# State-space rows, segments and decay products begin in their own group's last two slots; the modulation's multiply-adds one slot sooner in differential heads

## What is computed

```python
# differential attention, one of 8 heads
q = rope(rms_norm(q.reshape(B, S, H, 2, d), q_gain), positions)
k = rope(rms_norm(k.reshape(B, S, H, 2, d), k_gain), positions)
pr = jax.nn.softmax(sc, axis=-1)
w = pr[:, :, 0] - lam * pr[:, :, 1]
o = rms_norm(einsum(w, v), sub_gain) * (1.0 - lam_init)
y = o * jax.nn.silu(gate)
# modulation of the second block
mod = jax.nn.silu(c) @ w + b
# state-space layer, one of 8 groups of heads
acum = jnp.cumsum(ac, axis=1)
decay = jnp.exp(where(causal, acum[:, :, None] - acum[:, None, :], -inf))
y_diag = einsum("blsgk,bsgkp->blgkp", cb[..., None] * decay, xc)
y = (y + xs * D_skip) * jax.nn.silu(z)
yg = yg * rsqrt(mean(square(yg)) + eps)
return y @ out_w
```

## Time and profile before

| | us |
|---|---|
| median of three runs | 3638.04 |
| lowest, highest | 3634.32, 3638.28 |
| the profiled execution, whole | 3631.8 |
| its span in the trace | 3630.0 |
| TensorE busy in it | 3492.7 (96%) |
| VectorE busy | 2836.3 (78%) |
| ScalarE busy | 1948.7 (54%) |
| GpSimd busy | 579.3 (16%) |

### The profile page before, as it was taken

How to read it: one execution, slowest core, us unless ns; L and a number is a source line. 1 busy time by engine, 2 the same in 40 slices (tenths; PEclk the granted TensorE clock), 3 DMA queues, 4 the chain that set the end, 5 groups by cost and what they waited for, 6 DMA issues and landing times.

```text
span 3630.0 us, 68468 instructions
## 1 busy us (share of the span) xinstructions
PE 3492.7 (96%) x27986; PEld 3410.1 (94%) x27986; DVE 2836.3 (78%) x4649; ACT 1948.7 (54%) x3084; POOL 579.3 (16%) x546
## 2 busy tenths in 40 slices
PE   7999999999999999999999999999999998999997
PEld 7999999999899989999999999999999997999997
DVE  7787887677787887877877787898989866666665
ACT  6555546566547685565555456554545546434344
POOL 2111112111113011221111112231313300000000
PEclk9999999999999999999999999999999998999998
DMA  6555556434465444656555464445454443555552
GB/s 244 211 196 216 198 222 225 172 151 175 167 274 189 175 157 182 254 180 228 198 219 202 188 251 175 152 156 216 152 209 161 154 151 123 203 204 192 208 193 93
DMA packets 104904, 691.17 MB, mean 190 GB/s; under 512 B 12688, under 2 KB 21008, under 8 KB 22672
## 3 DMA queue, kind: packets, MB, share of 16 engines
q1 hardware_dynamic: 104128, 685.14, 50.9%
q0 software_dynamic: 464, 1.64, 0.1%
HBM read 676.25 MB, written 2.10 MB: 187 GB/s over the span
## 4 chain that ended last, share of the span: by engine, by line
PE 48%; DVE 15%; ACT 5%; issue 3%; POOL 1%; DMA 1%; SPq 0%; DVEq 0%; POOLq 0%; ACTq 0%
PE g L434 14%; PE g L436 14%; PE g L435 14%; DVE w_lo L1457 4%; ACT w_hi L944 2%; DMA scratch<-scratch 1%; POOL scratch L2271 1%; PE turn_bank L473 1%; DVE scratch L1987 1%; DVE con L1987 1%; DVE sq L1951 0%; DVE scratch L1958 0%; DVE sq L1950 0%; PE norm_bank L447 0%; DVE rstd L1950 0%
## 5 line engine op out<-in xcount | busy, mean ns | idle before, releaser
L1457 DVE TENSOR_TENSOR w_lo<-w_raw,w_hi 128x1024 fp32r<-128x1024 f32 x1088 | 1342.9, 1236 | 445.7 <-ACT w_hi L944 433.5
L944 ACT ACTIVATE w_hi<-w_raw 128x1024 fp32r<-128x1024 f32 x1088 | 1134.0, 1054 | 978.1 <-PE g L436 855.2
L434 PE MATMUL g<-p_hi,w_hi 128*128 128x256 f32 x4624 | 1333.0, 288 | 35.0 <-DVE w_lo L1457 23.1
L435 PE MATMUL g<-p_lo,w_hi 128*128 128x256 f32 x4624 | 1310.9, 283 | 0.0
L436 PE MATMUL g<-p_hi,w_lo 128*128 128x256 f32 x4624 | 1310.8, 283 | 0.0
L434 PE MATMUL g<-q_hi,w_hi 128*128 128x256 f32 x3472 | 1004.5, 289 | 18.4 <-DVE scratch L2164 10.5
L436 PE MATMUL g<-q_hi,w_lo 128*128 128x256 f32 x3472 | 986.3, 284 | 0.0
L435 PE MATMUL g<-q_lo,w_hi 128*128 128x256 f32 x3472 | 986.3, 284 | 0.0
L434 PEld LDWEIGHTS g<-p_hi,w_hi 128*128 128x128 f32 x4624 | 889.4, 192 | 49.5 <-DVE w_lo L1457 33.2
L435 PEld LDWEIGHTS g<-p_lo,w_hi 128*128 128x128 f32 x4624 | 889.7, 192 | 1.4
L436 PEld LDWEIGHTS g<-p_hi,w_lo 128*128 128x128 f32 x4624 | 889.2, 192 | 0.0
(11 more groups left out here) (421 smaller groups left out, 3833.1 us busy)
## 6 DMA issues: line engine op xcount, KB each, us to landing
w_raw<-in_slots SPq DMA_DIRECT2D x640, 1024.0 KB, 4.9
scratch<-scratch SPq DMA_DIRECT2D x128, 64.0 KB, 4.9
h<-in_x SPq DMA_DIRECT2D x4, 512.0 KB, 6.3
out_h<-h SPq DMA_DIRECT2D x4, 512.0 KB, 2.6
sq<-in_p POOLq DMA_DIRECT2D x4, 256.0 KB, 3.0
con<-in_consts SPq DMA_DIRECT2D x1, 832.0 KB, 10.9
scratch<-in_distance POOLq DMA_DIRECT2D x1, 576.0 KB, 5.6
vec<-in_vecs SPq DMA_DIRECT2D x1, 383.0 KB, 3.8
```

Source lines behind the costliest of these rows:

```text
L434: pe.matmul(g, wh, hi[:, k], start=n == 0, stop=False)
L435: pe.matmul(g, wh, lo[:, k], start=False, stop=False)
L944: act.activation(w_hi[k % SPLIT][:, cols], raw[MAIN_AT[k] % RAW][:, cols], ACT.Copy).then_inc(hi_ready, 1)
L1457: dve.tensor_tensor(w_lo[k % SPLIT][:, cols], raw[MAIN_AT[k] % RAW][:, cols], w_hi[k % SPLIT][:, cols], SUB).then_inc(lo_ready, 1)
```

## The change

In a differential head the modulation's halves move from the ends of bodies 2, 3, 6, 7 to the ends of bodies 1, 2, 5, 6; `mod_columns` moves from body 1, behind the turn, to body 0, and VectorE takes the columns in body 1 instead of 2. The modulation's blocks of these layers are loaded one place sooner.

In the state-space layer a group's rows, segments, decays and weights of `m = 0, 1` move into its own slots 8 and 9, and those of `m = 2, 3` from the next group's slots 2, 3 to its slots 0, 1. `s_out`, `s_y_out`, the squares and their sums move from steps 2 to 5 to steps 0 to 3, the norm from step 6 to 5, the scaling of y from 7 to 6, its low part from ahead of slot 8 to ahead of slot 7. The wait for the gate's last product at the group's end is taken apart: `s_y_out` waits for the one that it needs. After group 7 the steps beside the projection count from 0.

```diff
-    heads = lambda at: [at + 8 * n + m for n in range(A_HEADS) for m in (2, 6)]
+    heads = lambda at: [at + 8 * n + m for n in range(A_HEADS) for m in (1, 5)]
...
-                if j == 1 and prev:
+                if j == 0 and prev:
                     mod_columns([acc[:]])
...
         def s_previous(g, step, turned):
 
-            if 2 <= step <= 5:
-                s_out(step - 2, turned)
             if step < 4:
-                s_rows(g, step)
-            if step == 6:
+                s_out(step, turned)
+            if step < 2:
+                s_rows(g, step + 2)
+            if step == 5:
                 s_norm()
...
-            if g == S_GROUPS - 1:
-                s_previous(g, 0, None)
+                if n > 7:
+                    s_rows(g, n - 8)
...
         def s_previous(g, step):
+            if step < 2:
+                s_decay(step + 2)
             if step < 4:
-                s_decay(step)
-            if 2 <= step <= 5:
-                s_square(step - 2)
+                s_square(step)
+            if step == 5:
+                factor(rsn[:, 2], "eps_5")
             if step == 6:
-                factor(rsn[:, 2], "eps_5")
-            if step == 7:
                 s_y_hi(g)
...
-                g = take(columns=j == 2 and prev)
+                g = take(columns=j == 1 and prev)
...
-                if j in (2, 3, 6, 7):
-                    ada_half([acc[:]], (j - 2) % 4)
+                if j in (1, 2, 5, 6):
+                    ada_half([acc[:]], (j - 1) % 4)
...
-        def s_y_out(m):
+        def s_y_out(g, m):
 
             dve.wait_ge(yd_done, c.next("yd"))
+            dve.wait_ge(gluon, 10 * g + 7 + m)
...
         def s_previous(g, step):
-            if 2 <= step <= 5:
-                s_y_out(step - 2)
             if step < 4:
-                s_segments(g, step)
-            if step == 7:
+                s_y_out(g, step)
+            if step < 2:
+                s_segments(g, step + 2)
+            if step == 6:
                 s_scale_y(g)
...
-                if g and n == 8:
+                if g and n == 7:
                     s_y_lo(g - 1)
...
+                if n > 7:
+                    s_segments(g, n - 8)
                 if 4 <= n <= 7:
                     s_inputs(g, n - 4)
...
-            if g == S_GROUPS - 1:
-                s_previous(g, 0)
-            dve.wait_ge(gluon, c.at("gluon"))
...
         def s_previous(step):
+            if step < 2:
+                s_weights(step + 2)
             if step < 4:
-                s_weights(step)
-            if 2 <= step <= 5:
-                s_add_square(step - 2)
+                s_add_square(step)
...
+                if n > 7:
+                    s_weights(n - 8)
```

More of the change, by code:

```diff
@@ L799, in s_project @@
                 if tail:
-                    s_previous(S_GROUPS - 1, s + 1, turned)
+                    s_previous(S_GROUPS - 1, s, turned)
                 if s == 4 and i < 2:
@@ L1299, in s_group @@
                     s_previous(g - 1, n)
+                if n > 7:
+                    s_decay(n - 8)
             s_sigmoid(9)
-            if g == S_GROUPS - 1:
-                s_previous(g, 0)
         def s_project(tail=False):
@@ L1307, in s_project @@
                 if tail:
-                    s_previous(S_GROUPS - 1, s + 1)
+                    s_previous(S_GROUPS - 1, s)
         def norm_project(w):
@@ L2399, in s_group @@
                     s_previous(n)
+                if n == 8:
+                    c.next("cb")
+                if n > 7:
+                    s_weights(n - 8)
             s_silu(9)
-            c.next("cb")
         def layer_s():
@@ L2406, in layer_s @@
                 s_group(g)
-            for step in range(6):
+            for step in range(4):
                 s_previous(step)
```

## The result

| | before | after |
|---|---|---|
| median, us | 3638.04 | 3649.28 |
| lowest, highest, us (7 runs each) | 3634.32, 3640.78 | 3647.68, 3654.90 |
| span of the profiled execution, us | 3630.0 | 3645.9 |

The ratio is 1.0033, with a 95% interval of 1.0022 to 1.0044: the change makes the kernel some 12 us slower (11.2 by the medians), which is clear of noise. The time lies in the range given (3627 to 3653), but the forecast was no measurable change, 3641, and the range of the forecast itself ended at 3648. It came out as in the third rival, which had 3649.

A forecast was written before the change was run, and what follows sets the result against it. TensorE, busy 96% of the span, was taken as the bound, so only its waits count. Heads +11.3 and state-space -8.0 gave +3.3 us: 3641 against a median of 3638.04, no measurable change; range with rivals 3627 to 3653.

The forecast's parts named there:

- the third rival: Whole kernel slower: body 5's added half goes through whole, y's scaling eats the state-space gain; 3649 us, chance 0.22.
- The mechanism in the heads: Differential heads: the half entering body 5 delays VectorE's chain to the joined softmax and last scores; heads in all +11.3 us.
- the half taken from body 7: Differential heads, body 7: this modulation half was free, as VectorE idles 1.00 us for `w_hi` afterwards; removing it gains nothing.
- The delay of 0.93 us a head: TensorE's turn waiting for the joined softmax: body 5's added half costs 13.0 us over 14 heads.
- The order of SyncE's queue: Modulation loads in the heads, issued one place sooner: counted as nothing; a late transfer would show as a `w_hi` wait.
- The clock: Differential heads: longer turn waits cause one more fall of TensorE's granted clock, +1.0 us, bounds 0 and 8.
- The gain of the sum over the partitions: Differential heads: `mod_columns` moves ahead of the turn, hiding 0.37 us 14 times in its wait, -5.2 us.
- The state-space gain: Seven state-space groups: shorter VectorE chain, less later start and rows, gains net 1.1 us a group, 8 us in all.
- The start lag: State-space group's slot 0: VectorE's copy starts later behind TensorE, from 0.41 us to about 1.8.
- The chain from there: VectorE in a state-space group, slot 0's copy to slot 6's last scaled inputs: 50.6 us becomes 46.6.
- the segments, the two weight products and the scaling: State-space VectorE chain: segments leaving save 2.62 us, GpSimd weight products leaving save 2.66, scaling of y entering adds 2.15.
- The -0.9: State-space VectorE chain: fewer `w_lo` meetings with GpSimd's sum of squares, and other small ones, -0.9 us, between 0 and -1.6.

The follow-up runs named there:

- the heads alone: Only the differential heads changed, state-space layer as before, against the kernel before: 3647.72 against 3635.31 us, ratio 1.0034.

## Why the prediction was right or wrong

**The mechanism in the heads was right.** The half of the modulation put into body 5 goes through VectorE's chain to the turn and the scores; the last scores wait 10.0 us, as was said, and the turn 20.7 for some 22. Alone the heads cost 12.4 us for a forecast of 11.3. That the half taken from body 7 gained nothing by itself fits the waits, but no run moves it alone.

The delay of 0.93 us a head was 0.85 by the waits at the turn ((20.7 + 5.2 - 14.0) / 14). It also differs from head to head as was said. In the head with 2.43 us of idle time before line 1655 nearly none of it is left (VectorE's timeline after):

```profile
341.91 1.22 DVE L1457 TENSOR_TENSOR w_lo<-w_raw,w_hi 128x1024 fp32r<-128x1024 f32 x1
343.19 0.47 DVE L1655 TENSOR_TENSOR scratch<-scratch,sin_a 128x256 f32<-128x256 f32 x1
```

and the turn behind it waits 1.84 before and 1.44 after (TensorE's timeline, before, then after):

```profile
355.36 0.52 PE L473 MATMUL turn_bank<-con,scratch 128*128 128x128 f32 x3 [1.84 <-DVE scratch L1598]
```

```profile
359.57 0.52 PE L473 MATMUL turn_bank<-con,scratch 128*128 128x128 f32 x3 [1.44 <-DVE scratch L1598]
```

The 0.40 less is the sum over the partitions gone from behind the turn: this head got off, and so did the two others with about 2 us of idle time. After the change nearly every head waits the same 1.44.

**Three terms in the heads were off, and they nearly cancel.** The order of SyncE's queue was counted at nothing, with the words that a late transfer would show as a wait for `w_hi`. It showed as a wait for line 1657 instead: 4.0 us of new waits, and with the heads alone 4.6, none of which is left when the swaps stand ahead of the loads. The clock was given +1.0 for one more fall in the heads; there was none. And the half was rather overrated. Over all heads 14.8 us of idle time in bodies 6 became 0.4, so of 16 x 2.08 = 33.3 up to 18.9 could be left as delay; the heads alone say 12.4 + 5.2 = 17.6 with the queue in it, for 15.5 in the sum, and of these some 7 go when the swaps stand ahead of the loads. The two aren't parted further, for the half also covers part of the swaps' time. The gain of the sum over the partitions (-5.2) holds with the halves of the change (0.44 a head where it was taken as 0.37), and would have been nothing without them.

**The state-space gain was the step that failed**: -8.0, measured +3. In group 5 TensorE goes from slot 0's end to the turn that waits for slot 6's scaled inputs in 49.55 us (48.4 in the sum; before 51.0). The prediction calls this the turn of slot 6; it stands behind slot 7's matmuls, as the matmuls of line 784 right behind it tell, and waits for VectorE to have read the one before it. The stretch and its numbers are the same. The two ends after the change are in PE's timeline:

```profile
2772.18 0.66 PE L748 MATMUL out_bank<-scratch 128*64 128x256 f32 x4
...
2821.73 0.44 PE L473 MATMUL turn_bank<-con,vec 128*128 128x128 f32 x2 [1.97 <-DVE scratch L1976]
```

The start lag was right, 1.8 (2772.18 to the copy at 2773.97). The chain from there was 47.8, not 46.6: of the terms, the segments, the two weight products and the scaling came as said. The -0.9 came too, but not where it was looked for: `w_lo` takes 17.3 us in this stretch before and after, so its meetings with GpSimd did not go, and the 0.9 is smaller idle times and products of VectorE. What the sum lacked were new meetings with GpSimd, whose squares and gate products run beside other operations now: the second step of the convolution took 0.84 instead of 0.49 in two slots, and the first scaling of the inputs 0.83 instead of 0.35 in one slot more. That is 1.2 us. Rows of DVE and POOL in slot 4:

```profile
2805.34 0.83 DVE L1971 TENSOR_SCALAR scratch<-rstd,vec 128x256 f32<-128x256 f32 x1
```

```profile
2804.24 1.77 POOL L2366 TENSOR_TENSOR vec<-vec,sin_b 128x256 f32<-128x256 f32 x1 [2.56 <-ACT sin_b L992]
```

The Trainium skill's SBUF — State Buffer, section Who interferes with whom, lists `tensor_scalar` among the operations that can take the port pair shared with GpSimd, so that the one that comes second is held up. The trace agrees in kind: the operation takes 0.48 us longer beside the gate product, which had 0.67 left. The page's rule had been used in the prediction's sum for the meetings that go, and not for those that come.

The rest was on TensorE: the rows of slots 8 and 9 cost 1.6 us (1.5 in the sum), so that a group gained nothing (69.28 before, 69.48 after from turn to turn). The prediction's own terms say the same: 51.0 - 1.8 - 1.5 leaves no gain from a chain of 47.7 on (it had put this point at 48.0). And two of the waits of 1.98 were followed by a fall of TensorE's clock, which the sum had looked for in the heads and not here:

```profile
2380.00:2385.00 5.00, 4.91 (x27) 4.86 (x28) 4.96 (x9) 2.88 (x5) 1.54 (x1) 0.66 0.20 75
```

It makes the group from 2380 to 2451 1.5 us longer than its neighbours (71.00 for 69.48), and the other fall does the same. From the first group's turn to the last one's it is 2.4 us more than before, and 3.0 of it are these two falls. So of the 8 us forecast nearly all is missing without them, and the falls make the rest of the loss.

**The rival.** That its 3649 was met to the microsecond is luck: between the two traced executions the difference is 15.9 us, and by the medians 11.2. The slower rival named the added half going through whole and the scaling of y ahead of the inputs eating the gain. The place of the wait (up to 2.0 us, for slot 6's inputs) is as it was described. That the scaling is its cause was not confirmed: moved behind the inputs, it left the time the same.

## What to carry to other kernels

Before work is moved into a place where an engine waits for a transfer, look at what is issued just ahead of that transfer on its queue: here a 64 KB swap waited behind a 1 MB load, and changing that order was worth more than every move of arithmetic around it. Idle time on an engine's chain is a cover only once, and work put there keeps it from being won. Where one engine's chain is nearly as long as the bound engine's, a wait that is taken away comes back at the next place, so sum the chain over the whole period and look at each new meeting of two engines, not only at those that go.

## What the hardware showed

- A transfer of 64 KB within the core's memory landed some 2 us after its issue with the queue free (1.9 at least; 2.1 is the median of all of them with the swaps ahead of the loads), after 4.9 us as a median in the kernel before, where it stood behind a load of 1 MB, and after up to 8.6 where it stood behind three.
- TensorE's granted clock fell from its level of 2.4 GHz towards 1.2 GHz after single waits of 1.4 to 2.0 us, but not after all of them: of seven waits of 1.3 to 2.0 us at the turns after the change two, both of 1.98, were followed by it, and each cost about 1.5 us; after three others of 1.97 to 1.98 it did not fall.
